# Seven Strassen half products for pairs of tiles, and more of the expert tiles beside the top-k

## What is computed

```python
def peer_ffn(h, w_pq, sub_keys, u_emb, v_emb):
    q = (h @ w_pq).reshape(b, s, PEER_HEADS, 2, PEER_HALF)          # 8 heads, 2 halves of 128
    sc = jnp.einsum('bshpc,pnc->bshpn', q, sub_keys)                # 128 keys for each half
    top_v, top_i = lax.top_k(sc, PEER_TOPK)                         # 16
    cand = (top_v[..., 0, :, None] + top_v[..., 1, None, :])        # 16 x 16 sums
    best_v, best_i = lax.top_k(cand, PEER_TOPK)
    expert, gate = i1 * PEER_KEYS + i2, jax.nn.softmax(best_v)      # of 128 x 128 experts
    # over the chosen experts: gelu(u_emb[e] . h) * gate, then times v_emb[e]
```

## Time and profile before

| | |
|---|---|
| median of 3 runs (lowest to highest) | 5099.2 us (5095.26 to 5105.12) |
| time of the profiled execution | 5098.34 us |
| its span, first to last instruction | 5096.3 us |
| PE busy over the span | 4752.7 us, 93% |
| DVE / ACT / POOL busy | 2589.3 (51%) / 1625.7 (32%) / 1247.5 us (24%) |
| mean granted clock of TensorE | 0.963 |
| DMA engines' busy share, MB moved | 31.6%, 555.7 |

### The profile page before, as it was taken

One profiled execution on the slowest core, in us unless ns is written; L12 is line 12 of the kernel. 1 busy time (PEld: TensorE's weight loads), 2 busy tenths in 40 slices (PEclk: granted clock), 3 DMA queues, 4 the chain that ended last, 5 costly groups with the idle time before them and its releaser, 6 DMA issues. The chain is left out here.

```text
span 5096.3 us, 64146 instructions
## 1 busy us (share of the span) xinstructions
PE 4752.7 (93%) x22416; PEld 3784.9 (74%) x22416; DVE 2589.3 (51%) x4061; ACT 1625.7 (32%) x2575; POOL 1247.5 (24%) x754
## 2 busy tenths in 40 slices
PE   6999999976988979999989999999799999999998
PEld 5666666644767758888868888888588888888886
DVE  3777777784524235646564444444244444444444
ACT  3555555553413322222233333333211111111111
POOL 1444434431123012212111121121122222222221
PEclk8999999977999979999999999999899999999999
DMA  2111111104432122222224444444644343433341
GB/s 76 37 43 47 46 46 46 38 17 157 153 124 83 54 100 82 91 71 82 74 91 148 151 154 148 148 153 152 240 152 145 143 148 144 148 143 138 143 148 58
DMA packets 259767, 555.70 MB, mean 109 GB/s; under 512 B 15536, under 2 KB 146864, under 8 KB 257456
## 3 DMA queue, kind: packets, MB, share of 16 engines
q1 hardware_dynamic: 259632, 554.01, 31.6%
HBM read 384.60 MB, written 169.35 MB: 109 GB/s over the span
## 5 line engine op out<-in xcount | busy, mean ns | idle before, releaser
L149 PE MATMUL expert_o<-expert_ahi,expert_vhi 128*128 128x512 f32 x2048 | 798.4, 390 | 35.6 <-POOL expert_vlo L1998 31.3
L151 PE MATMUL expert_o<-expert_ahi,expert_vlo 128*128 128x512 f32 x2048 | 797.9, 390 | 0.0
L150 PE MATMUL expert_o<-expert_alo,expert_vhi 128*128 128x512 f32 x2048 | 797.9, 390 | 0.0
L2050 DVE TENSOR_TENSOR expert_acc<-expert_acc,expert_o 128x512 f32<-128x512 f32 x512 | 351.9, 687 | 737.8 <-PE expert_o L151 733.5
L1387 POOL TENSOR_TENSOR ulo<-uraw,uhi 128x1024 fp32r<-128x1024 f32 x128 | 311.2, 2432 | 1375.2 <-ACT uhi L1383 1375.2
L1998 POOL TENSOR_TENSOR expert_vlo<-expert_vraw,expert_vhi 128x1024 fp32r<-128x1024 f32 x128 | 323.7, 2529 | 1053.7 <-ACT expert_vhi L2016 1053.7
L149 PE MATMUL spread_a<-hhi,uhi 128*128 128x512 f32 x1280 | 505.7, 395 | 15.1 <-POOL ulo L1387 15.1
L151 PE MATMUL spread_a<-hhi,ulo 128*128 128x512 f32 x1280 | 499.8, 390 | 0.0
L150 PE MATMUL spread_a<-hlo,uhi 128*128 128x512 f32 x1280 | 498.8, 390 | 0.0
L149 PEld LDWEIGHTS expert_o<-expert_ahi,expert_vhi 128*128 128x128 f32 x2048 | 385.1, 188 | 117.3 <-issue 37.4
L1862 DVE TENSOR_TENSOR spread_one<-spread_iota,spread_parts 128x2048 f16<-128x2048 f16 x64 | 184.0, 2875 | 527.5 <-PE spread_g L1886 526.9
(11 more groups left out here) (288 smaller groups left out, 8583.8 us busy)
## 6 DMA issues: line engine op xcount, KB each, us to landing
uraw<-in_peer_u SPq DMA_DIRECT2D x128, 512.0 KB, 4.0
gelu_u<-ugelu SPq DMA_DIRECT2D x128, 512.0 KB, 2.9
gates<-spread_stage SPq DMA_DIRECT2D x16, 4096.0 KB, 17.1
expert_act<-gelu_u SPq DMA_DIRECT2D x128, 512.0 KB, 3.7
expert_graw<-gates SPq DMA_DIRECT2D x128, 512.0 KB, 4.5
expert_vraw<-in_peer_v SPq DMA_DIRECT2D x128, 512.0 KB, 6.4
mix_w_raw<-in_w_mix SPq DMA_DIRECT2D x56, 512.0 KB, 3.6
xattn_w_raw<-in_w_cross SPq DMA_DIRECT2D x32, 512.0 KB, 3.5
```

What stands on the lines that cost most here:

```text
L149: nc.tensor.matmul(out, whi, xhi, start=(first and i == 0), stop=False)
L150: nc.tensor.matmul(out, whi, xlo, start=False, stop=False)
L151: mm = nc.tensor.matmul(out, wlo, xhi, start=False, stop=(last and i == len(terms) - 1))
L2050: nc.vector.tensor_tensor(acc[:, k, h * H:h * H + H], acc[:, k, h * H:h * H + H], ops[:, d, h], ALU.add).then_inc(added, 1)
```

## The change

The query tiles and 92 instead of 48 expert tiles are computed in `select_phase`, as 54 pairs of tiles (8 pairs of queries, 46 of experts: one pair, then 6 for each of 8 heads, then 5). A pair is a 2x2 block matrix (2 tiles by 2 halves of the channels), as is the activation (2 halves of the channels by 2 halves of the tokens), and it is multiplied by Strassen's scheme in Winograd's form with 7 products of 4 chunks x 3 passes = 12 matmuls. The sums of weight blocks are made on POOL for each pair (`sums`), the sums of activation blocks once on DVE. Seven additions a pair are made on DVE out of four banks, and the top-k is cut into pieces between them. `raw_low` lies in the same memory as `raw`. The transposes of the selected experts stand in the middle of the last five pairs. `h`, the results of the top-k and the output blocks share buffers that live over both phases.

`spread_phase` keeps 36 tiles: four for each group of tokens, and four more behind the last. PE takes five half products, then four times two steps and one half product. Its two DMAs of gates are issued one behind the other. The last group of `v` runs over the first 512 tokens for all 8 chunks of channels and then over the others, with the norm and the output of the first half beside the products of the second.

```diff
-SELECT_TILES = 48
+PAIRS_PER_HEAD = 6
+QUERY_AT = 3
+TAIL_PAIRS = 5
+SELECT_TILES = 92
...
+        self.raw_low, self.s2_low, self.s14_low = [m.sb(f"{name}_low", shape, F32R) for name, shape in
+                                                   (("raw", [P, 2, 4, H]), ("s2", [P, H]), ("s14", [P, 2, 2, H]))]
+        self.raw, self.s2, self.s14 = [m.at(name, shape, F32, at + 4 * first) for name, shape, first in
+                                       (("raw", [P, 2, 4, H], 0), ("s2", [P, H], 8 * H), ("s14", [P, 2, 2, H], 9 * H))]
+        self.hi = m.sb("hi", [P, 7, H], F32R)
+        self.ps = m.ps("products", [P, 4, H])
...
+    def load(self, sync, n):
+        if n >= 2:
+            sync.wait_ge(self.done, self.NP * (n - 2) + 5)
+        sync.dma_start(self.raw[:, n % 2].rearrange("p b n -> p (b n)"),
+                       self.pairs_in[n].rearrange("p a c n -> p (a c n)")).then_inc(self.loaded[n % 2], 16)
+    def sums(self, pool, n, m, s):
+        a, g = self.raw[:, s], self.nc.gpsimd
+        pool.wait_ge(self.loaded[s], m * 16 + 16)
+        g.tensor_tensor(a[:, 2], a[:, 0], a[:, 2], ALU.subtract).then_inc(self.sum_made, 1)
+        if not (isinstance(n, int) and n == 0):
+            pool.wait_ge(self.done, n * self.NP - 4)
+        pool.wait_ge(self.sum_made, n * 4 + 1)
+        g.tensor_tensor(self.s2[:], a[:, 3], a[:, 2], ALU.subtract).then_inc(self.sum_made, 1)
+        pool.wait_ge(self.sum_made, n * 4 + 2)
+        g.tensor_tensor(self.s14[:, s, 0], a[:, 0], self.s2[:], ALU.add).then_inc(self.sum_made, 1)
+        g.tensor_tensor(self.s14[:, s, 1], a[:, 1], self.s2[:], ALU.subtract).then_inc(self.sum_made, 1)
+    def groups(self, s):
+        return ((self.raw[:, s, 0:2], self.hi[:, 0:2], self.raw_low[:, s, 0:2]), (self.s2[:], self.hi[:, 4], self.s2_low[:]),
+                (self.raw[:, s, 2:4], self.hi[:, 2:4], self.raw_low[:, s, 2:4]),
+                (self.s14[:, s], self.hi[:, 5:7], self.s14_low[:, s]))
+    def low(self, pool, n, s, g):
+        src, high, low = self.groups(s)[g]
+        if g == 0:
+            pool.wait_ge(self.sum_made, n * 4 + 4)
+        pool.wait_ge(self.hi_made, n * 4 + (g + 1))
+        self.nc.gpsimd.tensor_tensor(low, src, high.bitcast(F32), ALU.subtract).then_inc(self.lo_made, 1)
+    def high(self, act, n, m, s, g):
+        src, high, _ = self.groups(s)[g]
+        if g == 0:
+            act.wait_ge(self.loaded[s], m * 16 + 16)
+        else:
+            act.wait_ge(self.sum_made, n * 4 + (2, 2, 4)[g - 1])
+        if not (isinstance(n, int) and n == 0):
+            act.wait_ge(self.done, n * self.NP - (5, 4, 2, 0)[g])
+        self.nc.scalar.activation(high, src, ACT.Copy).then_inc(self.hi_made, 1)
...
+    def product(self, pe, n, s, j, made=None):
+        first = isinstance(n, int) and n == 0
+        if j != 1:
+            group = (0, None, 1, 2, 2, 3, 3)[j]
+            pe.wait_ge(self.lo_made, n * 4 + (group + 1))
+        if j == 0 and not first:
+            pe.wait_ge(self.added, n * self.NP - 3)
+        if j == 1 and not first:
+            pe.wait_ge(self.added, n * self.NP - 1)
+        if j == 2 and not first:
+            pe.wait_ge(self.added, n * self.NP)
+        if j == 3 and not first:
+            pe.wait_ge(self.added, n * self.NP - 4)
+        if j == 4:
+            pe.wait_ge(self.copied, n + 1)
+        if j == 5:
+            pe.wait_ge(self.added, n * self.NP + 2)
+        if j == 6:
+            pe.wait_ge(self.added, n * self.NP + 1)
+        bank = (0, 1, 2, 3, 0, 1, 2)[j]
+        high = self.hi[:, (0, 1, 4, 2, 3, 5, 6)[j]]
+        low = (self.raw_low[:, s, 0], self.raw_low[:, s, 1], self.s2_low[:], self.raw_low[:, s, 2], self.raw_low[:, s, 3],
+               self.s14_low[:, s, 0], self.s14_low[:, s, 1])[j]
+        b_hi, b_lo = [(h[:, 0], h[:, 2], t[:, 1], t[:, 2], h[:, 1], t[:, 0], h[:, 3])[j]
+                      for h, t in ((self.h_hi, self.t_hi), (self.h_lo, self.t_lo))]
+        for k in range(4):
+            if made:
+                pe.wait_ge(*made(k))
+            kp = slice(k * P, k * P + P)
+            mm = three_pass(self.nc, self.ps[:, bank], [(high[:, kp], low[:, kp], b_hi[:, k], b_lo[:, k])],
+                            first=(k == 0), last=(k == 3))
+        mm.then_inc(self.done, 1)
+    def add(self, dve, n, j):
+        tt, c, ps, count = self.nc.vector.tensor_tensor, self.block, self.ps, n * self.NP
+        dve.wait_ge(self.done, count + (j + 1))
+        if j == 2:
+            dve.wait_ge(self.copied, n + 1)
+            dve.wait_ge(self.freed[1], n * 16 + 1)
+            tt(c(1), c(0), ps[:, 2], ALU.add).then_inc(self.added, 1)
+            dve.wait_ge(self.added, count + 1)
+            tt(c(0), c(0), ps[:, 1], ALU.add).then_inc(self.added, 1)
+        elif j == 3:
+            dve.wait_ge(self.freed[3], n * 16 + 1)
+            dve.wait_ge(self.added, count + 1)
+            tt(c(3), c(1), ps[:, 3], ALU.add).then_inc(self.added, 1)
+        elif j == 4:
+            dve.wait_ge(self.freed[2], n * 16 + 1)
+            dve.wait_ge(self.added, count + 3)
+            tt(c(2), c(3), ps[:, 0], ALU.subtract).then_inc(self.added, 1)
+        elif j == 5:
+            tt(c(1), c(1), ps[:, 1], ALU.add).then_inc(self.added, 1)
+            dve.wait_ge(self.added, count + 4)
+            tt(c(3), c(3), ps[:, 1], ALU.add).then_inc(self.added, 1)
+        else:
+            dve.wait_ge(self.added, count + 5)
...
+def pair_kinds():
+    kinds = [0]
+    for hd in range(PH):
+        for i in range(PAIRS_PER_HEAD):
+            kinds.append(hd + 1 if i == QUERY_AT and hd < PH - 1 else None)
+    return kinds + [None] * TAIL_PAIRS
...
+            for n, kind in enumerate(KINDS):
+                def store(c):
+                    sync.wait_ge(pr.gelu, 4 * u + (1, 4, 2, 3)[c])
+                    sync.dma_start(a_out[2 * u + c // 2, :, c % 2 * H:c % 2 * H + H], pr.block(c)).then_inc(pr.freed[c], 16)
+                if kind is None:
+                    store(0)
+                if n + 2 < N:
+                    pr.load(sync, n + 2)
+                elif n == N - 2:
+                    sync.wait_ge(pr.done, 7 * n + 5)
+                    sync.dma_start(b12_raw, h12).then_inc(pr.loaded[n % 2], 16)
+                if kind is None:
+                    store(2)
+                    store(3)
+                    store(1)
+                    u += 1
...
+            dve.wait_ge(hlo_made, NC)
+            tt(B22, B22, B12, ALU.subtract).then_inc(t_made, 1)
+            dve.wait_ge(h12_stored, 16)
+            dve.wait_ge(t_made, 1)
+            tt(B12, B12, B11, ALU.subtract).then_inc(t_made, 1)
+            dve.wait_ge(t_made, 2)
+            tt(B11, B22, B11, ALU.add).then_inc(t_made, 1)
+            dve.wait_ge(t_made, 3)
+            tt(B21, B11, B21, ALU.subtract).then_inc(t_made, 1)
+            for x in range(4):
...
+            def body(hd, first, last):
+                def add(i, j):
+                    pr.add(dve, pair_of(hd, i)[0], j)
+                add(0, 2)
+                alone(dve, sc_made, hd * 2 + 2)
+                first_best(0, 8)
+                add(0, 3)
+                first_best(8, 16)
+                add(0, 4)
+                alone(dve, first8, hd * NU + NU)
+                find_and_cut(0, 3)
+                add(0, 5)
+                find_and_cut(3, 6)
+                add(0, 6)
+                if not first:
+                    gates(hd - 1)
+                find_and_cut(6, 9)
...
+                add(5, 2)
+                hits_index(hd, 0)
+                add(5, 3)
+                hits_sum(hd, 0)
+                add(5, 4)
+                hits(hd, 1)
+                add(5, 5)
+                hits_index(hd, 1)
+                add(5, 6)
+                hits_sum(hd, 1)
...
+        PER = 4
+        FIRST = 5
+        TILES = KEYS - SELECT_TILES
+        NS = 2
...
+            def gates(tt):
+                sync.wait_ge(staged, (tt + 1) * (STEPS * NB) + NB)
+                for i in range(NS):
+                    part = slice(i * KEYS // NS, (i + 1) * KEYS // NS)
+                    sync.dma_start(g_out[part].rearrange("a p t -> p a t")[:, :, tt * P:tt * P + P], stage[:, part, :]
+                                   ).then_inc(stored, 16)
+
+            for tt in range(NT):
+                for i in range(PER - 1):
+                    tile(tt * PER + i)
+                ex.load(sync, tt * PER + PER + 1)
+                gates(tt)
+                ex.store(sync, SELECT_TILES, tt * PER + PER - 1)
+            for n in range(PER * NT, TILES):
+                tile(n)
...
+                for i, h in halves[:FIRST]:
+                    half(i, h)
+                for st in range(0, STEPS, 2):
+                    for b in range(2):
+                        step(tt * STEPS + (st + b), b)
+                    for i, h in halves[FIRST + st // 2:FIRST + st // 2 + 1]:
+                        half(i, h)
+                for i, h in halves[FIRST + STEPS // 2:]:
```

(71 more changed lines are left out.)

807 lines of the change are left out of this document (469 added, 338 removed).

## The result

The changed kernel takes 5150.39 us (median of 4 runs, 5147.36 to 5152.54) against 5099.71 for the kernel before in the same session: ratio 1.0097, 95% interval 1.0084 to 1.011, so 1.0% slower. The profiled execution has a span of 5150.8 us against 5096.3.

A forecast was written before the change was run, and what follows sets the result against it. PE alone was taken to bound the select and spread phases. The terms -146.8 + 12 + 8 - 4 + 44 + 154 - 9 - 5 give +53 on 5098, so 5151 us, 1.0% slower; forecast range 5105 to 5190.

The forecast's parts named there:

- the pairs: Select phase: PE stays the bound, but top-k pieces on DVE wait for POOL, one us a head: +8 us.
- DVE in the spread stage: Spread phase: DVE's four operations a step and two collisions with POOL a group make PE wait: +44 us.
- Matmuls removed: 54 pairs of 84 matmuls replace 108 tiles of 48, 648 fewer at 0.2265 us each: -146.8 us.
- the select phase: Whole select phase: about 355 us longer, since expert tiles move into it.
- Start: Start of select: low parts of h, DVE's sums and POOL collisions delay the first pair's products: +12 us.
- the collisions named: Select pairs: DVE's candidate and hit pieces with two SBUF operands wait for POOL; taken as 8 us.
- Seam to spread: Between select and spread: the 24 transposes leave the end and cost about 4 us among the pairs: -4 us.
- the walk's 1.6 us: Spread phase: DVE slower than PE over four pairs of steps, 1.6 us of waiting a group without collisions.
- Load behind the gates: Spread phase: tile 2's load lands behind 8 MB of gates; PE idles 8 x 16.9 us, plus half clock: +154 us.
- Ends: Last gates land partly under the last tiles, -9 us; shorter DVE chain behind the last product, -5 us.
- The rival in which the load is in time: Spread phase: tile 2 lands within 21.8 us of the gates' issue, the 154 term is gone: 4997 us; chance 0.20.
- The other rivals: Waits half as long, 5072 us, chance 0.12; select bound by DVE and POOL, 5231, 0.08; clock not lowered, 5132.

The follow-up runs named there:

- run 10: Changed kernel, POOL computing one element of each low part in the select stage from the third pair on; output wrong: 5145.8 us.
- run 4: Changed kernel, POOL computing one element of each low part in the spread stage from its third tile on: 5105.78 us.
- run 6: Changed kernel, loads and stores reordered around and between gate transfers, second tile's low part held until DVE made the group's last gates: 5039.8 us.
- run 1: Changed kernel, load of the next group's tile 2 issued ahead of the gates: 5108.0 us.
- run 2: Changed kernel, that load and the store of the group's last tile both issued ahead of the gates: 5066.88 us.
- run 3: Changed kernel, each group writing only 4 MB of gates, the rest at the stage's end: spread stage 597.2 us, whole time 5153.6.
- run 7: Changed kernel, loads and stores of the spread stage issued on ACT's queue, SP issuing the gates alone: 5065.2 us.
- run 11: Kernel before with the new expert stage alone, last group of values by token halves: 5095.07 us against 5100.77.
- all four together: Changed kernel, three loads and a store ahead of the gates, a store between their transfers, a half product between paired steps: 5019.61 us.

## Why the prediction was right, step by step

The time, 5150.4, is 0.6 us from the forecast of 5151, and some of that is luck. Two terms, the pairs and DVE in the spread stage, are near in size for other reasons than given. The profiled execution began its select stage 6.0 us late, which no term has, and the other misses, 1 to 3 us each, sum up to some 5 us the other way. Below is each term with what the traces of before and after have for it.

- **Matmuls removed** (-146.8) and **the select phase**: +362.1 to its last product. The stage began 6.0 us later in this execution (SP's first issue 1848.10 against 1842.08), in code that the change leaves alone; first spread products lie between 2985.4 and 2993.7 over all runs with this select stage. Net +356, forecast +355.
- **Start** (+12): +15, by the second pair's first product at 1927.2, less the 6.0, against the 1908.5 of the earlier trace rows and the 2.7. The low parts of h end 2.3 us later than before (1896.7, less the 6.0, against 1888.4), where I had them end 2.4 earlier. The third product waits 11.9 us for DVE's sums and the first low part; the first of these sums stands beside an operation of POOL and takes 4.3 us in place of 2.3.
- **Pairs** (+8): +7 by difference, that is the net 356 less 332 for the 1464 matmuls that the stage has more, 15 for the start and 2.5 for the transposes. But it isn't the collisions named: run 10 prices those with the low parts at 1.3 us. The score matmuls take PE 37.2 us instead of 28.0; they now run in two pieces a head, with 5.1 us of idle time between and behind the pieces.
- **Seam to spread** (-4): -9.0 at the seam, and 2.5 for the 24 transposes among the pairs, so -6.5. Right in kind.
- **Spread, DVE** (+44): the stage less its products (391.4), its steps (121), the eight waits (137.4) and 17.4 of half clock behind them leaves 46.7, of which the stage before has 5.4 as well: +41. But PE waits for DVE once a group, 19.4 in all, not 5.5 a group: the walk's 1.6 us without collisions are 0.3 (run 4), and one of the two collisions hides (run 6). The rest is 9.1 of waits for ACT and 10.9 of half clock behind seven of the eight waits of 2.4 us. I had left these out and overrated the waits for DVE by as much.
- **Load behind the gates** (+154): 137.4 of idle time in eight waits (8 x 16.9 = 135 forecast) and 34.2 us from the gates' issue to ACT's start on the tile (32.8 forecast for the landing). The half clock behind each wait costs between 1.6 and 3.1 us, 17.4 in all (19 forecast). Together 155, as forecast. The prediction had the load wait in the queue; in fact SP doesn't issue it until 27.7 us after the gates. Runs 1, 2, 3 and 7 show the mechanism in four different ways. What the prediction didn't say is that the load is only the first of three: the store (11.9 us), the fourth load (8.1) and the gates' own landing (6.1) stand behind it, so that moving the load alone gives 42 us, not 154.
- **Ends** (-9, -5): -10.7 and -5.0 (+3.9 in the products, -8.9 behind the last addition), as worked out; run 11 measured 5.7 for the second.

The rival in which the load is in time is what a few lines of order give: without the waits of 17 us the change would have been a gain, 5067 in run 2 (the rival said 4997, without the two waits that come next). The other rivals fell: the waits were not half as long, PE waits for DVE's additions in the select stage for 2 us in all, and the clock did fall behind each wait of 17 us.

## What to carry to other kernels

When work is moved out of a stage, look at what it covered: here ten tiles lay over each 8 MB of gates and four remained, and the engine that bounds did not wait for the large transfer but for the small ones that stood behind it in SP's order. Put small loads and stores that someone waits for soon ahead of a large transfer, or on another engine's queue, and after each such edit ask what is late next, since the first fix here gave 42 us and all four together 131. A collision costs only if someone waits for the operation that it delays: of two a group one was free, and taking 71 us of such waits off DVE in the select stage gave 1.3.

## What the runs showed of the hardware

- SP itself is held behind a large transfer: its two issues of 4 MB took 13.1 us together, and the store behind them 14.5, so SP was free for the load 27.7 us after the first issue. At 290 GB/s 4 MB take 14.5 us and 8 MB 28.9, so SP comes free at about the time at which the bytes are gone; what exactly holds it no run shows. With nothing large ahead the issue of a load or store took 0.3 to 0.4 us. What stands in SP's program behind a large transfer is late by that, whatever its own size.
- Small transfers on ACT's queue pass a large one on SP's, 7.1 us from issue to use, and lengthen it by their bytes: in run 7 three loads and two stores, 512 KB each, are issued while the gates go, 8.4 + 2.6 MB in 36.3 us, which is 303 GB/s, about the rate of the gates alone (290).
- A cast on DVE of 256 elements, with one input in SBUF, took 2497 ns beside a busy POOL and 295 without its low parts. The prediction counted operations with two such inputs alone. The Trainium skill, "SBUF — State Buffer", section "Who interferes with whom", lists casts among those that can take the shared port as well, which I had passed over: its rule for operations with one SBUF input makes an exception of them. Additions with one input in PSUM took 688 and 687 ns in the mean, so they did not wait, as it says.
- A wait of 2.4 us before a step was followed by a stretch at the lower clock in seven of eight groups, and not in the first. In the second group the granted clock from 3128 to 3136 is 0.79, in the first, from 3043 to 3052, it is 1.00. The step itself took 2.36 us for 32 matmuls in the second group, 3.56 in the third and 1.96 in the first, and step and half product together lost 1.5 to 1.6 us each time.
